# Threshold searches of a sparse attention: three late blocks counted by ScalarE alone, x tiles turned earlier, bias rows stored head by head

## The chip, the cores and the metric

One core of a Trainium2 chip runs the whole kernel. The metric is the device time of one execution in microseconds (us), as the median of several runs. Engines: TensorE (PE, its weight load PEld), VectorE (DVE), ScalarE (ACT), GpSimd (POOL), SyncE (SP), whose queue issues most of the DMAs.

## The reference

One transformer block on 2048 tokens of width 1024: a norm and one projection `a @ w_in`, three mixers side by side (gated linear attention, a sparse attention "dsa", a sliding window "swa"), the output product, a mixture of 32 experts, an embedding term `e = rms_norm(p @ w_ple)` gated by the result, a last norm. The part that matters here is the choice of keys in the sparse attention:

```python
def block(inp):                       # one block of 128 queries
    j, qb, qib, wb = inp
    rel = relu(einsum('bthd,bsd->bths', qib, k_idx))      # 8 heads of width 64
    score = einsum('bth,bths->bts', wb, rel)
    score = where(key_pos <= t_pos, score, -inf)
    _, sel = lax.top_k(score, 256)                        # exact, ties by position
```

For each query the 256 highest scores among the keys before it are chosen. Blocks 0 and 1 need no choice; blocks 2 to 15 do, block j with 128 (j + 1) keys.

## The kernel before

The kernel runs in parts, each closed by a barrier of all engines. The change lies in the first, `project_and_select` (L116). It does three things at once.

**Projection.** 16 tiles of x are squared (ScalarE), scaled by the root (POOL makes it, L490, L492), turned by TensorE (L709) and copied with the gain by VectorE (L810, L815). TensorE then makes the products with `w_in` (L727 for 512 columns, L742 for token-major ones), ScalarE copies each to one of three stage buffers (L599, L608), SP's queue stores it (L439, L445). `order` is TensorE's list: X turns four tiles, M is a product, H its first half, R a score product (L757). Behind each half product stand two R.

**Scores.** For each R ScalarE takes relu (L618) and weighs two heads (L632), POOL adds them (L534, L537), with three `relu` buffers. When all pieces of a block are in, POOL hides its last diagonal square and signals `S_masked` (L547).

**Search.** For each block VectorE finds the 256th highest score bit by bit, in 32 rounds: `count` (L831) counts the scores at or above the trial value of each row, `lower` (L857) and `flip` (L864) make the next value. Blocks are searched in `GROUPS`: (2,3), (4,5), (6,7), (8,9,10,11), (12,13,14,15), so that the small operations are shared. In the last 8 bits of the fourth group and the last 31 of the fifth ScalarE counts two of the four blocks by a sum of signs (`sense`, L641), VectorE turns the sums into bits (L860). As signs miss ties, `settle` mends such thresholds with an own count (L876) and twelve small integer steps. Then ScalarE writes the side of every score (`tell`, L653) and VectorE's `pick` (L928 to L937) makes the mask, POOL stores it (L577). Early groups use `select` (L910 to L918) without ScalarE. The side tiles of blocks 8 to 11 lie in the `relu` buffers, so `tell` waits there for the last score piece; those of 12 to 15 lie over the scores of 8 to 11 and wait until these masks are stored. VectorE turns x tiles 12 to 15 between the first and the second group (`turned_over(LAST_X, NT)`).

The order in which ScalarE mixes its copies, score work and counts is written out beforehand by `deal()`: it walks through a rough time line with fixed costs (a count is 0.18 + 0.00104 times the width in us) and takes a count when ScalarE is free before its next item is due, with `LEAN` = 0.3 us of leave. VectorE's order is plain: group after group.

Around this: POOL fills the relative bias rows for 4 + 8 heads (L559 to L568) after the scores of blocks 2 and 3, and SP's queue stores them, 128 copies of 384 numbers a head, in two DMAs, one of four heads (from 4 partitions), one of eight, ahead of the stores of products from `("f", 5, 0)` on (L434). They are read again only at L1044 and L1045. Last comes the embedding: seven tiles of p are turned (L775) and multiplied with `w_ple` (L784); ScalarE copies the turned tiles (L677), squares and copies the results (L685, L687), and stores them (L689). In ScalarE's program all this stands behind everything in `act_order`, the last `tell` too.

Of the kernel before, what the change touches and what calls it, by code (L numbers as in the profile page):

```python
# [17 lines left out]
P = 128  # L18
# [62 lines left out]
GROUPS = [(2, 3), (4, 5), (6, 7), (8, 9, 10, 11), (12, 13, 14, 15)]  # L81
GROUP_OF = {j: g for g, js in enumerate(GROUPS) for j in js}
# [5 lines left out]
HELP_FROM = (-1, -1, -1, 7, 30)  # L88
HELPED = (0, 0, 0, 2, 2)
SEARCH_AT, LEAN, COUNT = 100.0, 0.3, 0.18  # L90
# [7 lines left out]
def width(j):  # L98
    return P * (j + 1)
# [16 lines left out]
def project_and_select(nc, outer, keep, home, near, x, g_mix, w_in, rel_bias, proj_f, proj_t, mask_dram, bias_rows, ident, ident_ready, layer_in, w_ple, e_dram, e_squares, operands):  # L116
# [3 lines left out]
    with body as ctx:  # L120
# [29 lines left out]

        sign_of = rank[:, :].bitcast(U8).rearrange("p (c n) -> p c n", c=2)
        tri, tri_big = sb("tri", [P, P]), sb("tri_big", [P, P])
        hidden_first = sb("hidden_first", [P, 2 * P], U8)
# [3 lines left out]
        flip = sb("flip", [P, 4], I32)  # L157
        cnt = sb("cnt", [P, 4])
        signs, sums = sb("signs", [P, 2]), sb("sums", [P, 4])
        ints = sb("ints", [P, 6, 2], I32)  # L160
        need = sb("need", [P, 2])
        raw_a, raw_s = sb("raw_a", [AH, NB_BUCKETS]), sb("raw_s", [SH, NB_BUCKETS])
        rows_a, rows_s = sb("rows_a", [AH, 384]), sb("rows_s", [SH, 384])
# [4 lines left out]
        lower = psX[:, 0, 0:4].bitcast(I32)  # L168
# [21 lines left out]
        flipped, sensed = sem("flipped"), sem("sensed")  # L190
# [5 lines left out]
        def side_of(j):  # L196

            if j >= LOW:
                return scores_of(S_low, S_high, j - 4).bitcast(F16)[:, 0:width(j)]
            return relu[:, :, :, :].rearrange("p b a n -> p (b a n)").bitcast(F16)[:, (j - 8) * 3 * CH:(j - 8) * 3 * CH + width(j)]  # L200
        pT = relu[:, 2, 0, :].rearrange("p (b k t) -> p b k t", b=2, k=KP)
# [68 lines left out]
        assert done == NREL and [i for k, i in order if k == "M"] == list(range(len(products)))  # L270

        SHARED = [g for g in range(len(GROUPS)) if HELP_FROM[g] >= 0]
        helped = [(g, b) for g in SHARED for b in range(HELP_FROM[g], -2, -1)]
        sensed_by, n = {}, 0
        for g, b in helped:
            if b >= 0:
                sensed_by[g, b] = n
                n += HELPED[g]  # L280
        LATE = [j for g in SHARED for j in GROUPS[g]]
        late = {j: i for i, j in enumerate(LATE)}

        halved = {o for o in order if o[0] == "H"}

        def deal():
            pe_at, pe_done, act_done = 0.0, {}, {}
            next_pe, act_at, pool_at, dve_at = 0, 25.0, 0.0, SEARCH_AT
            masked, flips, counted, late_x, out = {}, {}, {}, [], []
            steps = [(g, b) for g in range(len(GROUPS)) for b in range(NBITS, -2, -1)]  # L290
            next_step = 0

            def on_pe(k):

                nonlocal pe_at, next_pe
                while next_pe <= k:
# [8 lines left out]
                    elif kind == "R":  # L305
                        j, _, ci = pieces[i]
                        c0, c1 = chunks(j)[ci]
                        pe_at = max(pe_at, act_done.get(("R", i - NI), 0.0)) + 0.2 + 0.9 * (c1 - c0) / CH
                    pe_done[order[next_pe]] = pe_at
                    next_pe += 1  # L310

            def on_dve():

                nonlocal dve_at, next_step
                while next_step < len(steps):
                    g, b = steps[next_step]
                    js = GROUPS[g]
                    if (g, b) == (1, NBITS) and not late_x:
                        late_x.append(True)
                        dve_at += 11.0  # L320
                    if b == NBITS:
                        if any(j not in masked for j in js):
                            return
                        dve_at = max([dve_at] + [masked[j] for j in js]) + sum(COUNT + 0.00104 * width(j) for j in js) + 0.55
                    elif b >= 0:
                        shared = (g, b) in sensed_by
                        if shared and (g, b) not in counted:
                            return
                        dve_at += sum(COUNT + 0.00104 * width(j) for j in (js[0:len(js) - HELPED[g]] if shared else js))
                        dve_at = max(dve_at, counted.get((g, b), 0.0)) + 0.55  # L330
                        if b == 0 and HELP_FROM[g] >= 0:
                            dve_at += 2.5 + 0.5 + 0.00214 * width(js[3])
                    else:
                        dve_at += sum((1.4 + 0.0037 * width(j)) if HELP_FROM[g] >= 0 else (0.9 + 0.00625 * width(j)) for j in js)
                    if b >= 0:
                        flips[g, b - 1] = dve_at
                    next_step += 1

            ahead, k = list(helped), 0
            while k < len(order) or ahead:  # L340
                on_dve()
                ready = flips.get(ahead[0], 1e9) if ahead else 1e9
                if k < len(order) and order[k][0] in "XQH":
# [5 lines left out]
                    continue  # L349
# [2794 lines left out]
```

## Time and profile before

| | us |
|---|---|
| median of 3 runs | 2824.75 (2823.98 to 2826.58) |
| the profiled execution's own time | 2826.14 |
| span of its profile | 2824.4 |
| first part, up to the barrier | 841 |
| TensorE busy in the span | 2588.1 (92%) |
| VectorE / ScalarE / POOL busy | 1860.8 / 1259.8 / 927.4 |

The span runs from the first to the last instruction; the execution's time is 1.7 us longer. A timeline row merges equal instructions (x8) and gives in brackets how long the engine sat idle before it and what released it. A busy share over the whole span mixes parts with different limits; what the change is worth is read from the first part alone.

### The profile page before, as it was taken

What the parts mean: (1) busy time and instruction counts of PE and PEld (TensorE: products, weight loads), DVE (VectorE), ACT (ScalarE), POOL (GpSimd) and SP (SyncE); (2) the same over time, 40 slices, a digit from 0 to 9 for tenths busy, and PEclk for the clock granted to TensorE, in tenths of its full rate; (3) what the DMA queues carried; (4) which work ended last, traced back from release to release, by engine and by line L of the source; (5) the groups of instructions that cost most, each with busy time, mean ns of one, the idle gap of its engine ahead of it and who ended that gap; (6) DMA issues with size and microseconds to landing.
All of it is one profiled execution on the core that took longest, in us unless ns stands there. A gap on an engine that the chain in (4) does not pass through costs nothing. (4 is left out here: it accounts for less than half of the span.)

```text
span 2824.4 us, 35041 instructions
## 1 busy us (share of the span) xinstructions
PE 2588.1 (92%) x10908; PEld 1637.5 (58%) x10909; DVE 1860.8 (66%) x2646; ACT 1259.8 (45%) x2368; POOL 927.4 (33%) x925
## 2 busy tenths in 40 slices
PE   6999879999947889898899979999999999998998
PEld 3544424347823445444688756666666666665787
DVE  2389999979987788876333586644644444743676
ACT  2358667857956676766322222222222222222322
POOL 2377767810011111121000043434444444433221
PEclk9999989999967999999899989999999999999999
DMA  5202311122232223222544559975776665973663
GB/s 151 69 28 60 50 45 41 38 79 72 68 126 74 65 70 112 67 72 75 210 143 146 184 217 360 349 275 201 289 268 221 238 229 200 345 288 135 201 215 133
DMA packets 221475, 438.08 MB, mean 155 GB/s; under 512 B 22888, under 2 KB 91048, under 8 KB 221224
## 3 DMA queue, kind: packets, MB, share of 16 engines
q1 hardware_dynamic: 199400, 357.78, 36.9%
q0 software_dynamic: 13312, 47.32, 5.3%
q10 hardware_dynamic: 8640, 31.46, 2.8%
q8 instruction: 62, 1.02, 0.1%
q14 instruction: 61, 0.50, 0.1%
HBM read 331.14 MB, written 105.38 MB: 155 GB/s over the span
## 5 line engine op out<-in xcount | busy, mean ns | idle before, releaser
L2542 DVE CAST p_high<-p_low 128x2048 fp32r<-128x2048 f32 x128 | 203.2, 1587 | 400.8 <-PE p_psG L2649 293.0
L727 PE MATMUL p_psP<-home,p_ring 128*128 128x512 f32 x832 | 377.8, 604 | 11.3 <-DVE home L815 11.3
L2665 PE MATMUL p_psY<-p_wd,p_hT 128*128 x752 | 330.9, 593 | 2.2 <-ACT p_hT L2724 1.9
L2544 DVE TENSOR_TENSOR p_low<-p_low,p_high 128x2048 fp32r<-128x2048 f32 x128 | 318.9, 2492 | 4.4
L727 PEld LDWEIGHTS p_psP<-home,p_ring 128*128 128x128 f32 x832 | 153.8, 191 | 218.7 <-issue 206.1
L2665 PEld LDWEIGHTS p_psY<-p_wd,p_hT 128*128 128x128 f32 x752 | 139.3, 190 | 160.6 <-issue 160.5
L2585 POOL TENSOR_TENSOR p_xT_low<-p_xT,p_xT_high 128x512 fp32r<-128x512 f32 x94 | 186.0, 1997 | 3.3 <-ACT p_xT L2709 3.3
L2647 PE MATMUL p_psG<-p_high,p_xT_high 128*128 128x512 f32 x376 | 167.1, 444 | 15.7 <-DVE p_low L2544 8.0
L757 PE MATMUL p_psI<-p_kI,p_qI 64*128 64x512 f32 (+3 forms) x608 | 138.3, 574 | 27.7 <-ACT p_relu L618 26.2
L2591 POOL TENSOR_TENSOR p_hid<-p_act_g,p_act_u 128x512 f32<-128x512 f32 x47 | 62.1, 1321 | 308.2 <-ACT p_act_u L2719 295.3
L618 ACT ACTIVATE p_relu<-p_psI 128x1024 f32<-128x1024 f32 (+3 forms) x152 | 132.5, 914 | 64.3 <-PE p_psI L757 54.5
L2647 PE MATMUL p_psU<-p_high,p_xT_high 128*128 128x512 f32 x376 | 154.3, 410 | 5.6 <-DVE p_low L2544 5.6
L632 ACT ACTIVATE p_relu<-p_relu,p_small 128x512 f32<-128x512 f32 (+3 forms) x266 | 158.0, 664 | 0.0
L2730 ACT ACTIVATE p_y<-p_psY 128x512 f32<-128x512 f32 x94 | 56.2, 598 | 220.4 <-PE p_psY L2665 220.4
L2648 PE MATMUL p_psG<-p_low,p_xT_high 128*128 x376 | 150.3, 400 | 0.0
L2649 PE MATMUL p_psG<-p_high,p_xT_low 128*128 128x512 f32 x376 | 150.1, 399 | 0.0
L2648 PE MATMUL p_psU<-p_low,p_xT_high 128*128 x376 | 148.5, 395 | 0.0
L2649 PE MATMUL p_psU<-p_high,p_xT_low 128*128 128x512 f32 x376 | 148.5, 395 | 0.0
L2715 ACT ACTIVATE p_act_g<-p_psG 128x512 f32<-128x512 f32 x47 | 28.1, 598 | 261.9 <-PE p_psG L2649 261.9
L2719 ACT ACTIVATE p_act_u<-p_psU 128x512 f32<-128x512 f32 x47 | 28.1, 597 | 240.0 <-PE p_psU L2649 240.0
L641 ACT ACTIVATE p_rank<-p_S_high,p_flip 128x1920 uint8<-128x1920 f32 (+1 forms) x62 | 120.2, 1940 | 5.4 <-DVE p_flip L864 5.4
L757 PEld LDWEIGHTS p_psI<-p_kI,p_qI 64*128 64x128 f32 x608 | 53.0, 189 | 115.9 <-issue 81.1
(423 smaller groups left out, 5848.4 us busy)
## 6 DMA issues: line engine op xcount, KB each, us to landing
p_low<-in_w_expert_gate_dram SPq DMA_DIRECT2D x32, 2048.0 KB, 13.3
p_low<-in_w_expert_up_dram SPq DMA_DIRECT2D x32, 2048.0 KB, 18.1
p_wd<-in_w_expert_down_dram SPq DMA_DIRECT2D x32, 2048.0 KB, 10.7
y_dram<-p_y ACTq DMA_DIRECT2D x47, 512.0 KB, 7.9
p_xt<-in_x_dram SPq DMA_DIRECT2D x32, 512.0 KB, 4.6
y_dram<-p_clear SPq DMA_DIRECT2D x32, 512.0 KB, 4.4
proj_f<-p_stage SPq DMA_DIRECT2D x52, 256.0 KB, 2.4
p_ot<-o_dram SPq DMA_DIRECT2D x16, 512.0 KB, 4.3
```

The costliest lines, as they stand in the source:

```text
L618: act.activation(relu[:, n % NRELU, :, 0:c1 - c0], psI[:, n % NI, :, 0:c1 - c0], ACT.Relu).then_inc(relu_done, 1)
L632: act.activation(dst, src, ACT.Copy, scale=small[:, j, h:h + 1]).then_inc(weighed, 1)
L641: act.activation(sign_of[:, c, 0:width(j)], scores_of(S_low, S_high, j), ACT.Sign, scale=-1.0, bias=flip[:, own + c:own + c + 1].bitcast(F32),
L727: mm = pe.matmul(psP[0:n, i % 2, :], w, aT[:, k, c * CH:(c + 1) * CH], start=k == 0, stop=k == KD - 1)
L757: mm = pe.matmul(psI[:, n % NI, half, 0:c1 - c0], qI[r, b % 2, i, :], kI[r, c0:c1], start=True, stop=True)
L2542: dve.tensor_copy(high[:, m, k, :], low[:, par, m, k, :].bitcast(F32)).then_inc(high_done, 1)
L2544: dve.tensor_tensor(low[:, par, m, k, :], low[:, par, m, k, :].bitcast(F32), high[:, m, k, :].bitcast(F32), ALU.subtract).then_inc(w_split, 1)
L2585: pool.tensor_tensor(xT_low[:, k, :], xT[:, k, :], xT_high[:, k, :].bitcast(F32), ALU.subtract).then_inc(xT_split, 1)
L2647: pe.matmul(ps[:, :], xT_high[:, k, :], high[:, m, k, :], start=k == 0, stop=False)
L2648: pe.matmul(ps[:, :], xT_high[:, k, :], left, start=False, stop=False)
L2649: mm = pe.matmul(ps[:, :], xT_low[:, k, :], high[:, m, k, :], start=False, stop=k == KD - 1)
L2665: mm = pe.matmul(psY[:, c, :], hT[:, k, :], wd[:, bass.ds(at, 1), k, c * CH:(c + 1) * CH].rearrange("p a f -> p (a f)"), start=k == 0, sto ...
```

## The change

Groups are now (2,3), (4,5), (6,7), (8,9,10), (11,15). Blocks 12, 13 and 14 are `LONE`: VectorE makes the first count of each (`lone_start`), ScalarE all 31 others (`sense`, one block at a time), and VectorE turns each sum into a bit in two small operations (`lone_lower`, `lone_flip`), put between its own counts. `deal()` now writes out VectorE's order as well; among the counts that are ready ScalarE takes the block that is furthest behind. The group (11,15) is no longer helped or settled; only the lone blocks are settled, at the end, one by one, each with its own `tell` and `pick`. Picks of (8,9,10) and (11,15) follow their searches. Side tiles of 15, 12, 13, 14 lie over the scores of 8, 9, 10, 11, with one semaphore per stored mask. X tiles 12 to 15 are turned before group 0's search, on TensorE right after the score products of blocks 2 and 3. The bias rows are filled before the first scores; SP's queue stores one head behind each of the first twelve stores from `("f", 5, 0)` on. The embedding's steps P and E are part of `order` and are mixed with ScalarE's counts and tellings; their input overlays side tiles, so its load waits for the picks of blocks 8 to 10 (`FREED`).

```diff
-GROUPS = [(2, 3), (4, 5), (6, 7), (8, 9, 10, 11), (12, 13, 14, 15)]
+GROUPS = [(2, 3), (4, 5), (6, 7), (8, 9, 10), (11, 15)]
+LONE = [12, 13, 14]
+SIDE_IN = {15: 8, 12: 9, 13: 10, 14: 11}
-HELP_FROM = (-1, -1, -1, 7, 30)
-HELPED = (0, 0, 0, 2, 2)
-SEARCH_AT, LEAN, COUNT = 100.0, 0.3, 0.18
+PICKED = [j for js in GROUPS for j in js] + LONE
+TURN_LATE = 0
+SEARCH_AT, LEAN, COUNT = 100.0, 0.3, 0.25
...
-            if i == place[512, 2 * TPC]:
+            if done == first_rel[4, 0] and ("X", 3) not in order:
                 order += [("X", 3)]
...
+        order += [("P", 0)]
+        for i in range(EARLY):
+            order += [("P", i + 1)] * (i + 1 < EARLY) + [("E", i)]
...
+            def between(t):
+                for c, j in enumerate(LONE):
+                    if c not in next_bit:
+                        if masked.get(j, 1e9) <= t:
+                            dve_out.append(("S", c))
+                            t += COUNT + 0.00106 * width(j) + 0.55
...
+                    elif c in half_way:
+                        b = half_way.pop(c)
+                        dve_out.append(("F", (c, b)))
+                        t += 0.07
...
+                    elif sensed_at.get((c, next_bit[c]), 1e9) <= t:
+                        half_way[c] = next_bit[c]
+                        dve_out.append(("L", (c, next_bit[c])))
...
+                    for b in range(NBITS, -1, -1):
+                        for jj, j in enumerate(js):
+                            yield True, t
+                            t = between(t)
+                            dve_out.append(("N", (g, b, jj)))
+                            t += COUNT + 0.00106 * width(j)
+                        dve_out.append(("B", (g, b)))
+                        t += 0.4
...
+                allowed = [(t, w) for w, t in ready.items() if w[0] == "C" or k > LAST_R]
+                if allowed and max(min(allowed)[0], act_at) <= item + LEAN:
+                    soonest = max(min(allowed)[0], act_at) + 0.1
+                    t, what = max((a for a in allowed if a[0] <= soonest), key=lambda a: (a[1][0], a[1][1][-1] if a[1][0] == "C" else 0))
+                    del ready[what]
+                    act_at = max(act_at, t) + 0.05
+                    if what[0] == "C":
+                        act_at += 0.6 + 0.00077 * width(LONE[what[1][0]])
...
-                    for h0, n, rows in ((0, AH, rows_a), (AH, SH, rows_s)):
-                        sp.dma_start(bias_rows[h0:h0 + n, :, :], rows[:, :].unsqueeze(1).broadcast_to([n, P, 384])).then_inc(rows_stored, 16)
                 sp.wait_ge(copied, i + 1)
                 if p[0] == "f" and i in through:
...
                     sp.dma_start(proj_f[r0:r0 + n, ts(p[2], CH)], stage[0:n, q % NSTAGE, :]).then_inc(stored[q % NSTAGE], 16)
+                    h = i - place["f", 5, 0]
+                    if 0 <= h < AH + SH:
+                        row = rows_a[h:h + 1, :] if h < AH else rows_s[h - AH:h - AH + 1, :]
+                        sp.dma_start(bias_rows[h:h + 1, :, :], row.unsqueeze(1).broadcast_to([1, P, 384])).then_inc(rows_stored, 16)
...
                 if i == len(products) - 8:
                     sp.wait_ge(rel_done, NREL)
                     sp.wait_ge(summed, NREL)
+                    sp.wait_ge(chosen, FREED)
...
+            def sense(c, b):
+                j, col = LONE[c], 4 + c
+                act.wait_ge(lone_flipped, flipped_by[c, b])
+                if sensed_by[c, b] > 0:
+                    act.wait_ge(sensed, sensed_by[c, b])
+                act.activation(sign_of[:, 0:width(j)], scores_of(S_low, S_high, j), ACT.Sign, scale=-1.0, bias=flip[:, col:col + 1].bitcast(F32),
+                               accum_out=signs[:, c:c + 1]).then_inc(sensed, 1)
...
+            def lone_lower(c, b):
+                col = 4 + c
+                dve.wait_ge(sensed, sensed_by[c, b] + 1)
+                lowered[c] = chain(dve.tensor_scalar(lower[:, col:col + 1], signs[:, c:c + 1], float(width(LONE[c]) + 1 - 2 * TOPK), float(1 << b),
+                                                     ALU.is_gt, ALU.mult))
+            def lone_flip(c, b):
+                col = 4 + c
+                dve.wait_ge(step, lowered[c])
+                dve.scalar_tensor_tensor(out=flip[:, col:col + 1], in0=lower[:, col:col + 1], scalar=(1 << b) >> 1, in1=flip[:, col:col + 1],
+                                         op0=ALU.bitwise_xor, op1=ALU.bitwise_xor).then_inc(lone_flipped, 1)
...
-            for g in range(len(GROUPS)):
-                if g == 1:
-                    turned_over(LAST_X, NT)
-                search(g)
-                if HELP_FROM[g] >= 0:
-                    settle(g)
-                    pick(g)
-                else:
-                    select(g)
+            for kind, i in dve_order:
+                if kind == "X":
+                    turned_over(LAST_X, NT)
...
```

## Rows read from the trace of the kernel before

**Rows 1.** Busy times in windows: from:to us, length, each engine's busy us, clock, DMA share, GB/s.

```profile
121.00:841.00 720.00, 651.08 (x2149) 340.62 (x2147) 658.08 (x1266) 506.97 (x743) 337.51 (x360) 0.95 0.21 60
```

**Rows 2.** Timeline at the barrier: start us, us, engine line, operation, out<-in [idle before <-releaser].

```profile
829.34 2.35 DVE L937 SCALAR_TENSOR_TENSOR p_S_high<-p_rank,p_need,p_S_middle 128x2048 uint8<-128x2048 f16 x1
...
828.70 7.03 PE L784 MATMUL p_psI<-p_kI,p_relu 128*128 128x512 f32 x16
...
837.97 0.33 ACTq L689 DMA_DIRECT2D e_dram<-p_ring  x1
...
841.16 0.81 SPq L1281 DMA_DIRECT2D p_mask<-mask_dram  x2
```

**Rows 3.** Timeline of TensorE between its last products and the embedding.

```profile
744.83 28.22 PE L742 MATMUL p_psP<-p_ring,home 128*128 128x256 f32 x130
...
807.88 6.15 PE L784 MATMUL p_psI<-p_kI,p_relu 128*128 128x512 f32 x8 [31.73 <-ACT p_relu L677]
```

**Rows 4.** Busy times in windows: POOL before 91 us, and the x tiles 12 to 15.

```profile
60.00:90.00 30.00, 28.17 (x124) 20.06 (x123) 6.29 (x10) 2.43 (x8) 0.00 (x0) 1.00 0.30 104
...
187.72:206.07 18.35, 14.70 (x63) 8.31 (x63) 10.92 (x13) 9.82 (x16) 13.66 (x13) 0.89 0.09 29
```

**Rows 5.** Timeline around the start of the searches.

```profile
113.32 14.00 PE L727 MATMUL p_psP<-home,p_ring 128*128 128x512 f32 x32
...
121.39 0.55 DVE L831 TENSOR_SCALAR_CACHE_REDUCE p_above<-near 128x384 uint8<-128x384 f32 x1 [41.65 <-POOL near L547]
```

**Rows 6.** Timeline of TensorE around its gap in the score phase.

```profile
339.53 1.99 PE L757 MATMUL p_psI<-p_kI,p_qI 64*128 64x512 f32 x8
...
341.45 3.70 PE L727 MATMUL p_psP<-home,p_ring 128*128 128x512 f32 x8
...
365.82 3.60 PE L757 MATMUL p_psI<-p_kI,p_qI 64*128 64x512 f32 x8 [20.68 <-ACT p_relu L618]
```

**Rows 7.** Busy times in windows, while the bias rows are stored.

```profile
302.00:308.00 6.00, 6.00 (x22) 2.47 (x20) 5.79 (x13) 4.35 (x7) 5.69 (x7) 1.00 0.22 26
...
312.00:338.00 26.00, 26.00 (x79) 10.25 (x78) 25.06 (x55) 21.49 (x32) 22.95 (x21) 1.00 0.45 53
```

**Rows 8.** DMA issues up to 841 us: out<-in, queue, count, KB each, median us to landing.

```profile
proj_f<-p_stage SPq DMA_DIRECT2D x52, 256.0 KB, 2.4
```

**Rows 9.** Source L547, masking of the blocks: ns min/median/max, first to last start us.

```profile
L547 POOL TENSOR_TENSOR p_S_high<-p_tri_big,p_S_high x4: 455/462/468, 442.3 to 573.4; 128x128 f32<-128x128 f32 x4
```

**Rows 10.** Busy times in a window of the score phase, blocks 13 to 15.

```profile
442.00:570.00 128.00, 128.00 (x376) 50.22 (x375) 120.03 (x185) 105.41 (x155) 99.52 (x87) 1.00 0.14 42
```

**Rows 11.** Timeline of ScalarE: one sign pass.

```profile
692.47 1.90 ACT L641 ACTIVATE p_rank<-p_S_high,p_flip 128x1920 uint8<-128x1920 f32 x1 [0.26 <-DVE p_flip L864]
```

**Rows 12.** Timeline of VectorE: start of block 8's search; one bit of the last group.

```profile
401.42 1.35 DVE L831 TENSOR_SCALAR_CACHE_REDUCE p_above<-p_S_middle 128x1152 uint8<-128x1152 f32 x1 [0.46 <-POOL p_S_middle L547]
...
692.47 1.95 DVE L831 TENSOR_SCALAR_CACHE_REDUCE p_above<-p_S_high,p_flip 128x1664 uint8<-128x1664 f32 x1
...
694.34 2.07 DVE L831 TENSOR_SCALAR_CACHE_REDUCE p_equal<-p_S_high,p_flip 128x1792 uint8<-128x1792 f32 x1
...
696.53 0.21 DVE L860 TENSOR_SCALAR p_psX<-p_signs 128x1 int32<-128x1 f32 x2
...
696.97 1.95 DVE L831 TENSOR_SCALAR_CACHE_REDUCE p_above<-p_S_high,p_flip 128x1664 uint8<-128x1664 f32 x1
```

**Rows 13.** Timeline of VectorE: picks of the third group, own counts and picks of the last.

```profile
614.24 0.82 DVE L928 TENSOR_SCALAR p_equal<-p_S_middle,p_flip 128x1152 uint8<-128x1152 f32 x1
...
631.65 1.02 DVE L928 TENSOR_SCALAR p_equal<-p_S_middle,p_flip 128x1536 uint8<-128x1536 f32 x1
...
793.37 2.21 DVE L876 TENSOR_SCALAR_CACHE_REDUCE p_above<-p_S_high,p_flip 128x1920 uint8<-128x1920 f32 x1
...
800.10 1.08 DVE L928 TENSOR_SCALAR p_equal<-p_S_high,p_flip 128x1664 uint8<-128x1664 f32 x1
```

**Rows 14.** List of waits: who waited for whom, us in total, times, longest us.

```profile
DVE p_psX L860 <- ACT p_rank L641: 24.5, 17, 11.4
```

More of the change, by code:

```diff
@@ L308, in on_pe @@
                         pe_at = max(pe_at, act_done.get(("R", i - NI), 0.0)) + 0.2 + 0.9 * (c1 - c0) / CH
+                    elif kind == "P":
+                        pe_at = max(pe_at, act_done.get(("P", i - 2), 0.0)) + 0.4
+                    elif kind == "E":
+                        pe_at = max(pe_at, act_done["P", i], act_done.get(("E", i - 2), 0.0)) + 3.66
                     pe_done[order[next_pe]] = pe_at
                     next_pe += 1
-            def on_dve():
[L314 to L332, printed above, removed]
-                    else:
[L334 to L337, printed above, removed]
@@ L343, in deal, with let_dve @@
+            program, over = on_dve(), False
+            def let_dve(until):
+                nonlocal dve_at, over
+                while not over and dve_at <= until:
+                    go, t = next(program, ("over", dve_at))
+                    dve_at = t
+                    if go == "over":
+                        over = True
+                    if go is None:
+                        return
+            k = 0
+            while k < len(order) or not over:
                 if k < len(order) and order[k][0] in "XQH":
@@ L568, in _ @@
                 pool.tensor_copy(rows_s[:, at], raw_s[:, b:b + 1].broadcast_to([SH, n])).then_inc(filled, 1)
+            pool.wait_ge(filled, 2 + 2 * len(bucket_ranges()))
+            weigh_ready(0)
+            load_qI(2)
+            load_qI(3)
+            for t in range(LAST_X, NT):
+                inverse_root(t)
+            for j in (2, 3):
+                scored(j)
+            load_qI(4)
+            load_qI(5)
             for j in SCORED[2:]:
@@ new lines, in count, with count_bit @@
+                which = 1 - which
+                if junk_used[which]:
+                    dve.wait_ge(step, junk_used[which])
+                junk_used[which] = chain(dve.tensor_scalar((above, equal)[which][:, 0:W], scores_of(S_low, S_high, j), value, None,
+                                                           compare, ALU.add, accum_out=cnt[:, col:col + 1]))
+                return junk_used[which]
+            counted = 0
+            turned_bits = 0
+            def count_bit(g, b, jj):
+                nonlocal counted
+                j = GROUPS[g][jj]
+                if b == NBITS:
+                    dve.wait_ge(S_masked, j - SCORED[0] + 1)
+                    counted = count(jj, j, 0.0)
+                else:
+                    counted = count(jj, j, flip[:, jj:jj + 1].bitcast(F32))
@@ L862, in search @@
                     dve.wait_ge(step, at)
[L863 removed]
                     dve.scalar_tensor_tensor(out=flip[:, 0:n], in0=lower[:, 0:n], scalar=(1 << b) >> 1, in1=flip[:, 0:n],
                                              op0=ALU.bitwise_xor, op1=ALU.bitwise_xor).then_inc(flipped, 1)
[L866 to L877 removed]
+                dve.wait_ge(flipped, turned_bits)
@@ new lines, in _, with lone_start @@
+            lowered = {}
+            def lone_start(c):
+                j, col = LONE[c], 4 + c
+                dve.wait_ge(S_masked, j - SCORED[0] + 1)
+                at = count(col, j, 0.0)
+                dve.wait_ge(step, at)
+                at = chain(dve.tensor_scalar(lower[:, col:col + 1], cnt[:, col:col + 1], float(TOPK), -1.0, ALU.is_lt, ALU.mult))
+                dve.wait_ge(step, at)
+                dve.tensor_scalar(flip[:, col:col + 1], lower[:, col:col + 1], 1 << (NBITS - 1), None, ALU.bitwise_xor).then_inc(lone_flipped, 1)
@@ L878, in settle @@
+            def settle(c):
+                j, col = LONE[c], 4 + c
+                v, found = flip[:, col:col + 1], cnt[:, col:col + 1]
+                side, up, low, high, carried, change = (ints[:, i, :] for i in range(6))
+                dve.wait_ge(lone_flipped, flipped_by[c, -1])
+                count(col, j, v.bitcast(F32), ALU.is_gt)
                 at = chain(dve.tensor_scalar(side, v, 31, None, ALU.arith_shift_right))
@@ new lines, in _ @@
+            for kind, i in dve_order:
+                if kind == "X":
+                    turned_over(LAST_X, NT)
+                elif kind == "N":
+                    count_bit(*i)
+                elif kind == "B":
+                    next_values(*i)
+                elif kind == "S":
+                    lone_start(i)
+                elif kind == "L":
+                    lone_lower(*i)
+                elif kind == "F":
+                    lone_flip(*i)
+                elif kind == "Z":
+                    settle(i)
+                elif kind == "K" and i[0][0] >= MIDDLE:
+                    pick(*i)
+                elif kind == "K":
+                    select(*i)
```

392 lines of the change are left out of this document (206 added, 186 removed).

## The prediction

> **What bounds the kernel now.** I read the page first, then the busy times by stage, then each engine's timeline where the parts meet, last the list of waits. The first part of the kernel, all that the change touches, fills the span up to 841 us. From 121 us on VectorE is busy for 658 of 720 us: the threshold searches are one chain on it [rows 1]. The part ends in a barrier; the next part's first loads are issued at 841.16 us. Two ends meet there. VectorE's last mask is written at 829.34 + 2.35 = 831.69 us, and its store follows. ScalarE's last store of embeddings is issued later, at 837.97 us, 2.2 us behind the last embedding product (828.70 + 7.03 = 835.73), so this end sets the barrier [rows 2]. But it hangs on VectorE too: TensorE is through with the products at 744.83 + 28.22 = 773.05 us, and its embedding products begin only at 807.88 us, held by ScalarE [rows 3], whose program has the four side-tellings of the last group ahead of them, and those wait until VectorE has settled the thresholds, at 800.1 us. So VectorE's searches bound the part, and what matters is how far their end, and the embedding behind it, come forward.
>
> **The change, part by part.**
>
> **x tiles.** Tiles 12 to 15 cost VectorE 18.35 us between groups 0 and 1, of which it is busy 10.9 [rows 4], while it had sat idle for 41.65 us up to 121.39 us. After the change TensorE comes to them at 113.32 us, behind the score products of blocks 2 and 3 [rows 5]. Some 9 us of copies then end near 122.5 us, 1 us after the masks of group 0. VectorE gains 17 us. TensorE's work is only moved. The filling of the bias rows, 13.8 us on POOL, moves into 60 to 90 us, where POOL does nothing: free [rows 4].
>
> **Bias rows.** SP's queue gets two stores of bias rows near 300 us, and the stores of projections issued behind them land late: ScalarE waits, TensorE stands still for 20.68 us, and its next eight score products take 3.60 us instead of 1.99 (the lower clock level, 1.2 GHz) [rows 6]. That is 22.3 us. While they run, data moves at 26 GB/s with the four-head store alone and at 53 GB/s with the eight-head one beside it [rows 7]. The change issues one head, 192 KB, behind each of twelve product stores. In the score phase a product comes every 11 us (two times 1.99 for score products and 3.63 for half a product [rows 6]). A row costs at least what a product store of 256 KB costs, 2.4 us [rows 8]; by the 26 GB/s of four heads it costs 7.6 us; at most, if one head goes no faster than one of eight did (6.6 GB/s), 30 us. I take 7.6, the nearest row. With the product store that is 10, under 11, so it is hidden behind three stage buffers, and the whole 22.3 us leave TensorE's path. The Trainium skill (DMA: Bandwidth & Descriptors, Why a DMA increments its semaphore by 16 and not by 1) says that a copy runs on as many engines as divide its outermost dimension, thus 4, 8 and, afterwards, 16; by that alone a row would be at the lower end. The skill (SBUF — State Buffer, Door 1: The DMA port swizzle) speaks against that: four neighbouring partitions share a port, one sixteenth of 435 GB/s, by which a row takes 7.2 us. The steps of 26 and 53 GB/s agree with both pages.
>
> **Score phase.** Its last block is masked at 573.4 us [rows 9]; without the stall, at 551.1. New is that ScalarE counts for blocks 12, 13 and 14 inside it, from 420 us on. Late in this phase ScalarE is busy 105.4 of 128 us, TensorE 128 [rows 10]. A sign pass over 1920 elements takes 1.90 us [rows 11], so the 22.6 us of room hold 12; I take 12 to 15, and for each 0.4 us of hold-up on TensorE, as no row shows this mix (bounds 0 and 1.9: 0 to 28 us in all). Last mask near 557 us.
>
> **VectorE's searches.** In the last group a bit takes 4.50 us: 1.87 for 1664 elements, 2.00 for 1792, the rest 0.63, of which two small operations for ScalarE's blocks are some 0.13 [rows 12]. So a count is 1.87 and 0.13 more or less per 128 elements, and a bit's end 0.50. Blocks 8 to 10: 1.35 + 1.48 + 1.61 + 0.50 = 4.94, times 32 is 158 us. Blocks 11 and 15: 1.74 + 2.26 + 0.50 = 4.50, times 32 is 144 us. Three lone starts take 2.5 each, the 186 small operations of the lone blocks 0.07 to 0.2 each; I take 0.1: 4 us inside the first search, 15 in the second. That first search began at 401.0 us (401.42 less a wait of 0.46 [rows 12]), now 17 earlier: 384 + 158 + 7.5 + 4 = 553.5. Then the picks wait for the last score piece, as their side tiles lie in its buffers: first pick done near 560.3, and three picks take 17.4 us in all [rows 13]: 572.5 us. Blocks 11 and 15: 572.5 + 144 + 15 = 731.5. The four last picks take 31.6 us (800.10 to 831.69), so with 5.80 on average for blocks 8 to 10 a pick grows by 0.47 per block: 6.7 for block 11, 8.6 for 15, 23.0 for 12 to 14. 731.5 + 15.3 = 746.8. Blocks 12, 13, 14 one after another: counts 6.0, three times 2.4 of settling (793.37 to 800.10 holds two counts of 4.4 and one settling [rows 13]), picks 23.0: 783 us. For waits on ScalarE, to whose pace the two written orders tie VectorE, I add 7 us; the trace has 24.5 us of these, 11.4 of them one wait for the end of the score phase [rows 14]. VectorE ends at 790; its store, 2.4 us, and the barrier make it 794.5.
>
> **ScalarE's share.** Passes over 12, 13 and 14 are 1.7 + 1.8 + 1.9 = 5.4 us, with 10% for product copies 6 us a round. After 5 rounds in the score phase 26 are left: 156 us from 572.5, to 728, just before blocks 11 and 15 are through, and their picks' 15 us stand as slack.
>
> **The embedding**, next in line, now follows the products: 773.05 - 22.3 + 6 = 756.8, then 2.1 for the first turning, 27.85 (807.88 to 835.73) and 5.4 from there to the barrier: 792 us. It lies among tellings that wait for VectorE; I give that 3 to 5 us. Barrier at 797 instead of 841: **44 us less**. What follows starts from the same barrier, unchanged.
>
> The profiled execution took 2826.14 us, 1.7 more than its span and 1.4 above the median of 2824.75. 2826.1 - 44 = **2782 us**, 1.5% under the median.
>
> **The rivals.**
> - *The lone blocks come in late.* Each of their bits passes through both engines in an order fixed beforehand. For: the planner's formula (0.25 + 0.00106 times the width) gives a count of 1664 elements 2.01 us where the trace has 1.87 [rows 12], so VectorE reaches its waits before ScalarE does; the trace has 17 such waits [rows 14]. Against: the last group holds 4.50 us a bit with two passes in it. At 7 us a round the 26 rounds cost 26 more, less 15 of slack, and 4 for the embedding: 2797 us. Chance 0.20.
> - *Nothing holds.* No hold-up of the score phase, no extra waits: the embedding alone is the floor, 750.7 + 2.1 + 27.85 + 5.4 = 786, 55 less: 2771 us. Chance 0.12.
> - *The orders misfit altogether*, the counts move and spare nothing: 8.3 us a round are 60 more, less 15, which eats the 44: 2826 us. Chance 0.04.
> - *Slower: one partition is the limit.* If a head goes at 6.6 GB/s whoever reads it, a row takes 30 us; it decides from some 9 us on, where row and product store fill the 11. Twelve products then take 32 us each, 252 more, and the last score block and all behind it slip: -44 + 252 gives 3034 us. For: 26 and 53 GB/s are proportional to the heads. Against: heads, engines and partitions grow together there, so the rows can't part a limit of each partition from one of each engine or of four partitions together, and two of these three readings leave a row under 9 us. Chance 0.06. By the port rule named above it can't be.
>
> **The numbers.** The forecast case has 0.58 and its own range is 2775 to 2792 (hold-up 0 to 12 us, waits 0 to 10). With the late blocks and the floor case the range is 2764 to 2807: 7 us under the floor case for the clock in the next part, 10 above the late case. A measurement of this kernel can tell 0.2%, 5.6 us. Faster by more: 0.58 + 0.20 + 0.12 = 0.90; within it 0.03; slower 0.07 (one partition, and 0.01 for a worse misfit).
>
> **What would show it.** Right: TensorE without its gap at 345 us; a bias row landing in about 8 us; group 0's search from 122 to 124 us and no turning before group 1; last score mask at 550 to 560 us; embedding products from 759 us; barrier near 797. A step is wrong if TensorE idles more than 12 us in the score phase behind 420 us, if VectorE waits more than 20 us for sign passes, or if the embedding products stand apart while ScalarE waits for VectorE. The forecast fails if bias rows take over 9 us or the last pick ends after 805 us.

## The result and the profile after

The changed kernel takes 2791.23 us (2789.94 to 2792.84), the kernel before, on the same chip, 2825.44 us (both are medians of four runs). The ratio is 0.9879, 95% interval 0.9862 to 0.9897, 34 us less. The profiled execution after took 2789.94 us, its span is 2788.2 us, 36.2 less than before.

| | before | forecast | after |
|---|---|---|---|
| time, us | 2825.4 | 2782 | 2791.2 |
| barrier of the first part, us | 841.2 | 797 | 802.8 |
| last score mask | 573.4 | 557 | 545.4 |
| search of blocks 8 to 10 begins / ends | – | 384 / 553.5 | 394.5 / 567.8 |
| TensorE's last product ends | 773.1 | 756.8 | 743.7 |

The whole first part in windows (from:to us, length, each engine's busy us, clock, DMA share, GB/s), to be held against [rows 1]:

```profile
121.00:803.00 682.00, 647.19 (x2134) 336.64 (x2132) 628.40 (x1351) 529.40 (x774) 322.49 (x294) 0.98 0.29 64
```

The same part takes 38 us less, VectorE has 30 us less work in it, ScalarE 22 us more, and VectorE still fills 628 of 682 us. The timeline at the barrier of the changed kernel (L763 is the embedding's store, L1059 the last step of a pick):

```profile
773.50 0.33 ACTq L763 DMA_DIRECT2D e_dram<-p_ring  x1
...
794.83 2.22 DVE L1059 SCALAR_TENSOR_TENSOR p_S_high<-p_rank,p_need,p_S_middle 128x1920 uint8<-128x1920 f16 x1
...
802.76 0.81 SPq L1413 DMA_DIRECT2D p_mask<-mask_dram  x2
```

Before, the embedding's last store came 6 us behind the last mask and set the barrier [rows 2]. Now it is issued at 773.5 us, 21 us ahead of the start of the last mask's writing. The embedding's last product ends at 771.2 us. VectorE's chain alone ends the part. What follows the barrier gives back 2.2 us (38.4 us at the barrier, 36.2 in the span).

The first view shows the stores of bias rows in the changed kernel (DMA issues: queue, count, KB, median us to landing), the second the masks of the late blocks (source L630: ns min/median/max, first to last start):

```profile
bias_rows<-p_rows SPq DMA_DIRECT2D x12, 192.0 KB, 8.8
```

```profile
L630 POOL TENSOR_TENSOR p_S_high<-p_tri_big,p_S_high x4: 454/464/472, 414.9 to 545.4; 128x128 f32<-128x128 f32 x4
```

A row lands in 8.8 us (forecast 7.6 for itself), and TensorE has no gap at 345 us. The score phase ends 28.0 us sooner than in [rows 9]; the gap of [rows 6] accounts for 22.3. The rest was in a second gap of the kernel before, which the forecast left out (TensorE stood 5.5 us, and the next eight score products took 3.79 us instead of 1.99). With single rows in the kernel before, nothing else changed (b_newrows below), TensorE stands 1.6 us near there. The timeline before:

```profile
405.68 3.79 PE L757 MATMUL p_psI<-p_kI,p_qI 64*128 64x512 f32 x8 [5.52 <-ACT p_relu L618]
```

The search of blocks 8 to 10 and their first pick in VectorE's timeline (against [rows 12, 13]):

```profile
394.48 1.35 DVE L927 TENSOR_SCALAR_CACHE_REDUCE p_equal<-p_S_middle 128x1152 uint8<-128x1152 f32 x1
...
567.81 0.82 DVE L1049 TENSOR_SCALAR p_equal<-p_S_middle,p_flip 128x1152 uint8<-128x1152 f32 x1
...
573.36 0.21 DVE L1054 TENSOR_SCALAR p_need<-p_rank,p_sums 128x1 f32<-128x1 f16 x1 [2.13 <-ACT p_relu L744]
```

It starts 10.5 us later than forecast and lasts 173.3 us instead of 169.5. The pick then waits 2.1 us for a telling, ahead of which ScalarE takes two counts and a product copy.

Last, VectorE's waits in the changed kernel from 123 to 795 us, without that one for the telling (who waited for whom, us in total, times, longest us):

```profile
DVE p_above L927 <- POOL near L630: 15.3, 1, 15.3
DVE p_psX L977 <- ACT p_sign_of L729: 5.5, 7, 1.7
DVE p_above L927 <- POOL p_S_high L630: 4.5, 2, 3.5
```

The 24.5 us for sign passes of [rows 14] are down to 5.5. But a wait of 15.3 us is new. It stands ahead of block 5's first count, at the time at which VectorE turned x tiles before.

### The profile page after: what moved, and what is told of

Read it like the earlier page. It is cut to its first block and busy times, and to the rows that moved or that the text cites. A ratio compares the mean times of both kernels' runs of the same rounds, so it can differ in the third digit from the quotient of the medians.

```text
span 2788.2 us, 35407 instructions
## 1 busy us (share of the span) xinstructions
PE 2582.5 (93%) x10908; PEld 1636.0 (59%) x10909; DVE 1840.7 (66%) x2741; ACT 1281.8 (46%) x2398; POOL 932.0 (33%) x925
## 5 line engine op out<-in xcount | busy, mean ns | idle before, releaser
L729 ACT ACTIVATE p_sign_of<-p_S_high,p_flip 128x1664 uint8<-128x1664 f32 (+2 forms) x93 | 165.9, 1784 | 6.2 <-DVE p_flip L984 2.3
L1664 PE MATMUL p_psX<-p_kA,near 64*128 64x512 f32 (+3 forms) x320 | 86.5, 619 | 53.3 <-ACT near L1545 42.4
```

What stands on the lines that cost most here:

```text
L729: act.activation(sign_of[:, 0:width(j)], scores_of(S_low, S_high, j), ACT.Sign, scale=-1.0, bias=flip[:, col:col + 1].bitcast(F32), accum_ ...
```

## The experiments

All ratios are to the kernel before on the same chip; "barrier" is the start of the `p_mask` loads in the profiled execution, as in [rows 2]. The expectation of each run names two theories, A and B; the text behind it says which one the run bears out.

| run | time, us | ratio | 95% | barrier |
|---|---|---|---|---|
| b_newrows | 2801.8 | 0.9909 | 0.9894 to 0.9924 | 816.6 |
| b_spread | 2803.6 | 0.9919 | 0.9902 to 0.9936 | 815.0 |
| b_earlyx | 2829.6 | 1.0009 | 1.0000 to 1.0018 | 843.5 |
| a_oldrows | 2822.6 | 0.9984 | 0.9975 to 0.9993 | 832.6 |
| a_latex | 2790.3 | 0.9871 | 0.9856 to 0.9886 | 802.0 |
| a_pairs | 2794.4 | 0.9885 | 0.9869 to 0.9902 | 803.5 |
| a_settle | 2786.6 | 0.9861 | 0.9844 to 0.9877 | 796.7 |
| a_settle_lean | 2785.2 | 0.9854 | 0.9837 to 0.9870 | 796.8 |
| a_best_latex | 2790.3 | 0.9876 | 0.9861 to 0.9891 | 801.9 |
| a_best_020 | 2793.4 | 0.9891 | 0.9875 to 0.9907 | 807.1 |
| a_best_count | 2801.8 | 0.9919 | 0.9905 to 0.9932 | 815.1 |
| a_best_032 | 2802.6 | 0.9926 | 0.9912 to 0.9940 | 816.2 |

### The bias rows alone, on the kernel before: b_newrows

```diff
-                    for h0, n, rows in ((0, AH, rows_a), (AH, SH, rows_s)):
-                        sp.dma_start(bias_rows[h0:h0 + n, :, :], ...
...
+                    h = i - place["f", 5, 0]
+                    if 0 <= h < AH + SH:
+                        sp.dma_start(bias_rows[h:h + 1, :, :], ...
```

> The kernel before with the bias rows stored head by head behind twelve product stores, nothing else. Theory A: VectorE bounds the part, and only its wait of 11.4 us for the end of the score phase can go: 2825 - 11 = 2814 us, TensorE's products 20 us earlier and its idle time ahead of the embedding 12 us longer. Theory B: what leaves TensorE leaves the time: 2825 - 22 = 2803 us.

Theory A falls, and B's 2803 us come out. The time is 25.7 us less and the barrier comes 24.5 us sooner, although VectorE was the busy engine. The list of waits shows how (against [rows 14]):

```profile
DVE p_psX L862 <- ACT p_rank L643: 3.2, 8, 1.8
```

All but 3.2 of the 24.5 us were consequences of the stall. Besides the one wait of 11.4 us, there was a trail of five waits of 1.4 to 1.8 us behind it. One of them in the kernel before, in VectorE's and in ScalarE's timeline:

```profile
582.26 0.16 DVE L860 TENSOR_SCALAR p_psX<-p_signs 128x1 int32<-128x1 f32 x1 [1.83 <-ACT p_rank L641]
```

```profile
580.18 0.60 ACT L599 ACTIVATE p_stage<-p_psP 128x512 f32<-128x512 f32 x1 [3.27 <-PE p_psP L727]
```

ScalarE's written order has the copy of a product ahead of the counts. TensorE was late with its products, ScalarE stood 3.3 us for one, and VectorE waited for the count behind it. Some 3 us more come from the start of the search of blocks 8 to 11 (398.55 instead of 401.42 us). Only 0.5 of them were a wait for a mask; the rest lies in VectorE's own selects of blocks 6 and 7 (the last operation over 1024 elements took 1.36 instead of 2.17 us), and why was not tested. So nearly the whole stall reached the end of the part.

The changed kernel's barrier is another 13.9 us earlier than this run's. VectorE's last mask is written 9.8 us sooner (797.05 instead of 806.81 us), and the embedding, which here still ended behind it, gives 4.1. How the 9.8 us divide between the lone blocks, the new groups and the written order was not tested.

### The bias rows undone, in the changed kernel: a_oldrows

> The changed kernel with the bias rows in two stores again (four heads, eight heads, ahead of the products' stores). Theory A, the written order passes the stall on: TensorE stands still for some 21 us near 345 us, the masks of blocks 12 to 14 come 22 us later, and as VectorE's fixed order has their first counts at set places, where it already waits 3.5 us now, VectorE stands there for some 20 us: 2791 + 20 = 2811 us. Theory B, VectorE's own work hides it: only the first pick waits for the late last score piece (567 instead of 545, against a search that ends at 567.8), plus its sign pass: 2791 + 2 to 8 = 2793 to 2799 us. The prediction's sum, by which the 22 us leave TensorE's path alone, is B.

The edit is the one above the other way round (the eight rows of the second store lie in partitions 32 to 39 here, in 0 to 7 in the kernel before). Theory A holds in its mechanism, and the price is greater than its 20 us: 2822.6 us, some 31 above the changed kernel (30 by the ratios, as the two ran on different chips), barrier 29.8 us later. The timelines of TensorE and of VectorE in this run:

```profile
366.52 3.78 PE L845 MATMUL p_psI<-p_kI,p_qI 64*128 64x512 f32 x8 [23.23 <-ACT p_relu L705]
```

```profile
443.23 1.89 DVE L925 TENSOR_SCALAR_CACHE_REDUCE p_above<-p_S_high 128x1664 uint8<-128x1664 f32 x1 [30.97 <-POOL p_S_high L628]
```

VectorE stands at block 12's first count for 31.0 us, because its written order puts that count ahead of its own next one. In the changed kernel the same wait is 3.5 us. Without the single rows, the rest of the change is worth 5 us, and with them some 8 (0.9909 against 0.9879). The stall costs 30 us in the new order and 26 in the old; TensorE's gap is 23.2 us long here, 20.7 in the kernel before, which explains no more than a part of the difference.

### What a bias row is bound by: b_spread, and two rows at once: a_pairs

```diff
-        rows_a, rows_s = sb("rows_a", [AH, 384]), sb("rows_s", [SH, 384])
+        rows_a, rows_s = sb("rows_a", [4 * AH, 384]), sb("rows_s", [4 * SH, 384])
...
-                        sp.dma_start(bias_rows[h0:h0 + n, :, :], rows[:, :].unsqueeze(1)...
+                        sp.dma_start(bias_rows[h0:h0 + n, :, :], rows[0:4 * n:4, :].unsqueeze(1)...
```

> The kernel before with each bias row held four times over, in four neighbouring partitions, and its two stores (four heads, eight heads) reading every fourth partition; DMAs, bytes and their heads as before (the twelve rows are loaded with twelve small DMAs). Theory A, four neighbouring partitions share one way out at some 26 GB/s: four times the rate, the two stores take under 15 us instead of 36, TensorE's gap of 20.7 us goes, 2802 us as with single rows. Theory B, an engine or a partition gives 6.6 GB/s: 26 and 53 GB/s as before, the gap stays, 2827 us.

Each row lies in four neighbouring partitions, and twelve small DMAs load them so. Theory A holds: 2803.6 us, and no gap of TensorE from 300 to 400 us (busy 99.9 of 100 us). The same two DMAs, read from every fourth partition, in a window of this run:

```profile
302.00:308.00 6.00, 6.00 (x21) 2.32 (x19) 5.73 (x14) 4.34 (x7) 5.52 (x8) 1.00 0.49 184
```

Where the kernel before moved 26 GB/s [rows 7], this one moves 184; b_newrows, whose first row is issued at 309.8 us, moves nothing in that window, so both figures are the bias rows alone. This decides between the three readings that the prediction left open: heads and DMAs are the same, so neither a head's partition nor its engine gives only 6.6 GB/s; the four neighbouring partitions together were the limit. The Trainium skill (SBUF — State Buffer, Door 1: The DMA port swizzle) says that four neighbouring partitions share one port; the trace agrees, with 26 against 184 GB/s.

```diff
-                    h = i - place["f", 5, 0]
-                    if 0 <= h < AH + SH:
+                    for h in (2 * (i - place["f", 5, 0]), 2 * (i - place["f", 5, 0]) + 1):
+                        if 0 <= h < AH + SH:
```

> The changed kernel with two heads behind each of six product stores instead of one behind each of twelve. A row takes 8.7 us from issue to landing now. Theory A, rows of one group of four partitions can't overlap (26 GB/s together): two take 15 us or more, and with the product's own store that is 17.5 against the 11 us between products, 6.5 us over for each of six, less what two spare stage buffers hold (22 us): TensorE loses 10 to 17 us, 2800 to 2808 us. Theory B, the landing time is mostly latency and two rows overlap: no gap, 2791 us.

The DMA issues of this run, the rows (300 to 400 us) and the five product stores issued among them (317 to 375 us):

```profile
bias_rows<-p_rows SPq DMA_DIRECT2D x12, 192.0 KB, 16.4
...
proj_f<-p_stage SPq DMA_DIRECT2D x5, 256.0 KB, 13.9
```

Rows do not overlap (16.4 us where one alone takes 8.8), as A has it, and yet there is no gap: 2794.4 us, the same as the changed kernel within the intervals, barrier 0.8 us later. The rows did hold up the product stores: these landed in 12.5 to 18.2 us, where they take 2.4 beside single rows. But ScalarE never waited for a stage buffer in this run, while it waited 24.7 us for one in the kernel before. A's working was wrong where it added the product's own 2.4 us to two rows of 7.5. The twelve rows took some 89 us with the product stores among them (308 to 397 us), 7.4 each, so a pair takes 14.8 against the 11 us between products: 4 us a product, some 23 for six, about what two spare buffers hold (22 us). The threshold is not at 11 us a product for so short a run of rows.

### The x tiles: a_latex and b_earlyx

```diff
-TURN_LATE = 0
+TURN_LATE = 1
...
-            if done == first_rel[4, 0] and ("X", 3) not in order:
+            if i == place[512, 2 * TPC]:
```

This is the edit of a_latex. In b_earlyx the kernel before gets the same two steps the other way round: X 3 early on TensorE, `turned_over` ahead of group 0.

> The changed kernel with x tiles 12 to 15 turned after group 0's search again, and on TensorE back behind the products that block 4 waits for. Theory A: the early turning only moved VectorE's idle time, because the masks of blocks 4 and 5 come 8 us later for it (VectorE waits 15.3 us for the mask of block 5); group 1 starts near 206 instead of 202.3 us: +4 us, 2795 us. Theory B, the prediction's: VectorE loses 17 us, 2808 us.

> The kernel before with x tiles 12 to 15 turned ahead of group 0's search, on both engines, nothing else. Theory A: the mask of block 5 comes later, and the 4 us that are left are lost at the masks of blocks 8 to 11, which come at 400.6 us, when VectorE was only just there before: no change, 2825 us (2822 to 2827). Theory B, the prediction's: VectorE gains 17 us, 2808 us.

Theory A is the nearer one twice, and even its 4 us don't show: undone in the changed kernel 2790.3 us (0.9871 against 0.9879), done alone on the kernel before 2829.6 us, which is 2 us more than the kernel before on that chip (2827.5), not less. First the mask of block 5 in the kernel before, then that mask and VectorE's first count of block 5 in the changed kernel:

```profile
193.93 0.47 POOL L547 TENSOR_TENSOR near<-p_tri_big,near 128x128 f32<-128x128 f32 x1
```

```profile
201.84 0.47 POOL L630 TENSOR_TENSOR near<-p_tri_big,near 128x128 f32<-128x128 f32 x1
...
202.34 0.95 DVE L927 TENSOR_SCALAR_CACHE_REDUCE p_above<-near 128x768 uint8<-128x768 f32 x1 [15.32 <-POOL near L630]
```

TensorE's turning now stands ahead of the products that block 4 needs, so the mask of block 5 comes 7.9 us later, and VectorE waits for it instead of turning. In b_earlyx, where nothing else is changed, that mask comes 5.9 us later (199.81 us) and VectorE waits 15.6 us. By then VectorE has made only block 4's first count (at 186.19 us). The second bit of group 1 begins at 203.73 instead of 208.19 us: 4.5 us of the 17. In a_latex the search of blocks 8 to 10 begins 4.7 us later than in the changed kernel (399.2), yet ends 1.9 us sooner (565.9): it meets no wait for masks of late blocks. The lead had been spent there. In b_earlyx VectorE meets a wait of 3.9 us for the masks of blocks 8 to 11, and 30.8 us of waits for sign passes, 18.7 of them the one for the end of the score phase (11.4 before): what it gained early it waits for late.

### The three lone blocks settled together: a_settle and a_settle_lean

```diff
-ints = sb("ints", [P, 6, 1], I32)
+ints = sb("ints", [P, 6, len(LONE)], I32)
...
-                v, found = flip[:, col:col + 1], cnt[:, col:col + 1]
+                v, found = flip[:, 4:4 + len(LONE)], cnt[:, 4:4 + len(LONE)]
...
+                    if g == len(GROUPS) - 1:
+                        dve_out.append(("Z", 0))
```

> The changed kernel, but the three lone blocks are settled together, right behind the search of blocks 11 and 15 and ahead of all picks; the twelve small steps run once over three columns. Theory A, VectorE's chain still sets the end: two of three settlings of 2.4 us go, and their picks wait no longer for tellings: the last mask is written some 5 us earlier, 2791 - 5 = 2786 us. Theory B, ScalarE sets the end there (its last count is through at 744.4 us, 1.4 us ahead of VectorE's): the settling waits for it and the embedding's steps stand between the tellings: no change, 2791 us.

2786.6 us, last mask 6.1 us sooner (788.74 instead of 794.83 us). Theory A holds. But 1.9 of these 6.1 us are there when the search of blocks 8 to 10 begins (392.62 instead of 394.48 us), ahead of all that the edit changes. 4.2 are its own; two settlings of 2.4 us would be 4.8.

```diff
-                if allowed and max(min(allowed)[0], act_at) <= item + LEAN:
+                if allowed and max(min(allowed)[0], act_at) <= item + (LEAN if k <= LAST_R else 1.2):
```

> As a_settle, and behind the score phase ScalarE may start a count when a product copy is due within 1.2 us instead of 0.3. In the changed kernel ScalarE sits idle for 0.74 us in each round of 6.91 us, waiting for a product. Theory A: the written order costs VectorE its 4.6 us of waits for counts; they go, 3 to 4 us under a_settle. Theory B: VectorE's own work between the picks is the bound and ScalarE's speed is nothing to it: as a_settle, with TensorE's products ending 1 to 3 us later.

The edit aims at ScalarE's idle time ahead of a product copy, once in each round. In its timeline in the changed kernel:

```profile
705.74 0.39 ACT L697 ACTIVATE p_stage<-p_psP 128x256 f32<-128x256 f32 x1 [0.74 <-PE p_psP L832]
706.02 1.78 ACT L729 ACTIVATE p_sign_of<-p_S_high,p_flip 128x1792 uint8<-128x1792 f32 x1
```

2785.2 us, the fastest of all; but the barrier is that of a_settle (796.84 and 796.67 us) and the 1.4 us lie within the intervals. Theory B holds: ScalarE's last count comes 3.5 us sooner (738.9 instead of 742.5 us) and nobody is waiting for it. Against the changed kernel both are 5 to 6 us less by their medians, with intervals that overlap a little. The barrier comes 6 us sooner in both.

### The written order: a_best_latex, a_best_count, a_best_020, a_best_032

All four are a_settle_lean with one edit: the x tiles as in a_latex, or another fixed cost of a count in the planner. The planner then writes out both orders anew, so two of these kernels differ in more than one place of the order.

> As a_settle_lean, with x tiles 12 to 15 turned after group 0 again, as in a_latex. There the search of blocks 8 to 10 began 4.7 us later than in the changed kernel (399.2 against 394.5) and yet ended 1.9 us sooner (565.9 against 567.8), as it met no wait for the masks of late blocks. Theory A: that 1.9 us carries through: 2783 us. Theory B: ScalarE's counts end later too, and the settling, which now waits for all of them, takes it back: 2785 to 2788 us. The prediction's value for the x tiles, 17 us, would give 2802 us.

Theory B holds in its mechanism, a little above its 2788 us, with 2790.3: ScalarE's last count moves from 738.9 to 748.9 us, and VectorE waits 13.6 us for counts. The early x tiles, worth nothing in the changed kernel, are worth some 5 us in this one (0.9876 against 0.9854, with intervals that overlap).

```diff
-SEARCH_AT, LEAN, COUNT = 100.0, 0.3, 0.25
+SEARCH_AT, LEAN, COUNT = 100.0, 0.3, 0.14
```

> As a_settle_lean, with the planner's fixed part of a count at 0.14 us instead of 0.25, so that its count of 1664 elements is 1.90 us (trace: 1.87). Theory A, the written order is the cost: the first counts of the lone blocks stand later in VectorE's order and its 11 us of waits (4.5 for masks of late blocks, 6.8 for sign passes) shrink by half or more: 5 us less, 2780 us. Theory B: the order only moves the waits, as VectorE and ScalarE are both nearly full up to 745 us: no change, 2785 us.

> As a_settle_lean, with the planner's fixed part of a count at 0.20 us. At 0.25 VectorE waits 4.5 us for masks of late blocks and 6.8 for counts; at 0.14 ScalarE's last count ended at 762.2 instead of 738.9 us, as only 10 instead of 14 counts lay ahead of 545 us, and VectorE waited 28.0 us. Theory A, an optimum lies between: the first counts stand two bits later in VectorE's order, its wait of 3.5 us goes, ScalarE's last count ends near 742 us, still ahead of VectorE: 2781 us. Theory B, each bit by which the lone blocks start later is lost to ScalarE, which is full: its last count ends at 748 us or later and 2788 us or more result.

> As a_settle_lean, with the planner's fixed part of a count at 0.32 us, so that its VectorE is slower than the true one by 0.2 us a count. Theory A, the written order puts the first counts of the lone blocks earlier than their masks can come: VectorE waits longer there (8 us or more instead of 4.5), ScalarE's last count does not end sooner than 738.9 us: 2788 to 2792 us. Theory B, VectorE's slack at the masks takes it: no change, 2785 us.

| COUNT, us | time, us | VectorE waits for masks / counts | counts begun by 545.5 us | ScalarE's last count |
|---|---|---|---|---|
| 0.14 | 2801.8 | 0 / 28.0 | 10 | 762.2 |
| 0.20 | 2793.4 | 0.4 / 20.6 | 11 | 754.2 |
| 0.25 | 2785.2 | 4.5 / 6.8 | 14 | 738.9 |
| 0.32 | 2802.6 | 12.6 / 15.7 | 13 | 747.1 |

The planner that fits VectorE's true cost best (0.14) is 17 us slower than the one that overstates it. Theory A for a_best_count fell in size and sign, and B's "no change" with it. In a_best_020 B holds, while for a_best_032 A holds and its price is again too small. The lists of waits for 0.14, VectorE's and ScalarE's (400 to 780 us), and VectorE's timeline for 0.32:

```profile
DVE p_psX L980 <- ACT p_sign_of L732: 28.0, 13, 5.2
```

```profile
ACT p_sign_of L732 <- DVE p_flip L987: 24.1, 29, 2.4
ACT p_sign_of L732 <- DVE p_flip L974: 11.7, 2, 10.5
```

```profile
416.34 1.89 DVE L930 TENSOR_SCALAR_CACHE_REDUCE p_equal<-p_S_high 128x1664 uint8<-128x1664 f32 x1 [11.36 <-POOL p_S_high L633]
```

With 0.14 the first counts of the lone blocks stand late in VectorE's order, and ScalarE's order has its own counts at places that VectorE doesn't reach in time. ScalarE waits 35.8 us in all until VectorE has a trial value for it; with 0.25 that is 0.9 us. In return it waits 17 us less for products. The longest of these waits, 10.5 us up to 430.3 us, holds up the score work behind it too: TensorE stands 8.4 us, and the last score mask comes at 556.6 instead of 544.8 us. All 28 us of VectorE's waits for counts are at the end: its last own count is through at 729.2 us, ScalarE's at 762.2. Each engine waits for the other in turn. Of the 23 us by which ScalarE's last count comes later, 19 are idle time and 4 are work that now stands ahead of it (54.2 us idle from 400 us on instead of 35.2, 308.2 us busy instead of 303.9). With 0.32 the first counts stand too early: VectorE stands still at masks for 12.6 us and for counts 15.7, and its search of blocks 8 to 10 ends at 583.5 instead of 566.5 us. That is where nearly the whole loss arises. It was not tried why the middle lies at 0.25 and not at the true cost: the planner's other costs were left alone.

## Why the prediction came out right, point by point

The range and the sign held, and the value was 9 us off. VectorE's end came at 797.05 instead of 790 us: 10.5 us from the start of the search of blocks 8 to 10, 3.8 from its length, nothing net from all that follows, less the 7 us of waits that were set aside for it. The store and the barrier took 5.7 us instead of 4.5.

That the value came so near is in part luck. Two shares of the sum were wrong by about as much in opposite directions: the x tiles were to give 17 us and gave none of the time, the stall was to cost VectorE 11.4 us and its removal alone gave 25.7. The 7 us set aside for waits took up most of what was left.

- *VectorE bounds the part:* right, and after the change it does so alone.
- *Bias rows, 7.6 us each and hidden:* right. A row lands in 8.8 us, and rows taken two at a time take 7.4 each. One partition is not the limit: it alone gave 22 GB/s, not 6.6. (The half product that the step puts at 3.63 us is 3.70 in [rows 6]; the 11 us stand.)
- *The stall is 22.3 us of TensorE's path:* right for the gap named, short by 5.5 us for the second gap at 405.68 us.
- *What of the stall VectorE feels:* the step took 11.4 us, the one long wait, as the stall's, and kept 7 us of the other waits for the changed kernel. This term was too small: b_newrows shows that 21.3 of 24.5 us went with the stall, and 3 more ahead of the search of blocks 8 to 11. Rows alone give 25.7 of the 34 us.
- *x tiles, VectorE gains 17 us; "TensorE's work is only moved":* this step failed. It is moved ahead of what group 1 waits for. The gain was 4.5 us at group 1, and none in the time. It is the main reason that blocks 8 to 10 began at 394.5 instead of 384 us, the largest error of the sum.
- *Score phase held up by 6 us:* not at all. The last mask came at 545.4 us, and with the second gap gone that is no hold-up. It cost nothing in the sum, as the search lasted longer.
- *Search of blocks 8 to 10, 169.5 us:* 173.3, of which 4.5 are waits for masks of late blocks, a place that the prediction did not price. a_latex, without them, has 166.7.
- *Blocks 11 and 15, 159 us; picks 15.3; lone blocks 36:* 157.8, 15.5 and 35.7. Here each term came straight from a row.
- *7 us of waits on ScalarE, and 3 to 5 for the embedding:* VectorE waited 5.5 us for counts and 2.1 for a telling. The embedding was no near tie but 21 us early, since the products ended 13 us sooner than forecast.
- *Lone blocks late (0.20) and misfit orders (0.04):* did not happen at 0.25, but a_best_020 and a_best_032 show, on a_settle_lean, that 0.05 us less in the planner's constant costs 8 us and 0.07 more 17. The argument for this rival was one-sided: it took the overstated count for the danger, which a_best_032 bears out, while a truer count (0.14) cost as much by leaving ScalarE idle.

## What to carry to other kernels

Work moved into an engine's idle time is free only if the other engine that shares it doesn't reach it ahead of what the next wait is for: read what stands behind it in both queues. When a stall goes, look for its trail in the list of waits; small waits behind a long one can belong to it (here 10 of 13 us). The cost that a planner assumes when it writes out the order of two full engines is a tuned constant: try it on both sides of the value, and don't expect the truest cost to be the best one.

## What the runs showed of the hardware that was not expected

Reading the same twelve heads with the same two DMAs from every fourth partition raised the rate from 26 to 184 GB/s in the same window. A single row's 192 KB from one partition took 8.8 us (22 GB/s), so one partition gives nearly what four neighbours give together. Twelve such rows issued in pairs took 7.4 us each, and the product stores of 256 KB issued among them landed in 12.5 to 18.2 us, against 2.4 beside single rows: the rows held them up.
